# Shift and scale terms of the first norm both as matrix-vector products on TensorE, and the start's low parts and square sums on VectorE

## The reference

```python
def adaln_terms(s, w, b):
    return jnp.split(jax.nn.silu(s) @ w + b, N_MOD, -1)

def modulate(h, g, shift, scale):
    return rmsnorm(h, g) * (1 + scale) + shift

def swiglu(x, w_up, w_down):
    gate, up = jnp.split(x @ w_up, 2, -1)
    return (jax.nn.silu(gate) * up) @ w_down
```

## Time and profile before

| | us |
|---|---|
| three runs, median | 3085.34 |
| lowest, highest | 3085.33, 3086.22 |
| the profiled execution | 3084.96 |
| its span | 3083.2 |
| TensorE busy in it | 2977.2 |
| VectorE, ScalarE, GpSimd busy | 1601.4, 985.1, 997.4 |
| first dense product, start of the steady ones | 25.81, 76.55 |

### The profile page before, as it was taken

One profiled execution on the slowest core, in us unless ns is written; L12 is line 12 of the kernel. 1 busy time (PEld: TensorE's weight loads), 2 busy tenths in 40 slices (PEclk: granted clock), 3 DMA queues, 4 the chain that ended last, 5 costly groups with the idle time before them and its releaser, 6 DMA issues.

```text
span 3083.2 us, 45849 instructions
## 1 busy us (share of the span) xinstructions
PE 2977.2 (97%) x19023; PEld 2788.4 (90%) x19023; DVE 1601.4 (52%) x2437; ACT 985.1 (32%) x1701; POOL 997.4 (32%) x516
## 2 busy tenths in 40 slices
PE   7999999999989988999999999999999999999998
PEld 6999999999888875899999999999999877798997
DVE  6556666784646656477667684212123348431223
ACT  4211212343454457321121232212122247532222
POOL 5333333333332202233333333222222222344442
PEclk8999999999999999999999999999999999999999
DMA  4434454323320022234444342111211210132222
GB/s 189 147 112 133 126 143 130 98 75 125 111 66 15 8 80 78 78 126 137 130 134 145 103 131 69 62 62 59 64 62 55 75 47 2 62 102 90 90 95 70
DMA packets 126236, 284.25 MB, mean 92 GB/s; under 512 B 40222, under 2 KB 57550, under 8 KB 126030
## 3 DMA queue, kind: packets, MB, share of 16 engines
q1 hardware_dynamic: 123150, 274.86, 27.6%
q10 hardware_dynamic: 2880, 6.47, 0.5%
HBM read 269.68 MB, written 15.10 MB: 92 GB/s over the span
## 4 chain that ended last, share of the span: by engine, by line
PE 89%; DVE 5%; ACT 4%; issue 2%; POOL 0%; DMA 0%; ACTq 0%; SPq 0%; DVEq 0%; POOLq 0%
PE psum L1777 78%; PE psum L1952 2%; PE psum L2052 1%; DVE o_acc L1604 1%; PE psum L2040 1%; ACT prob_o L1258 1%; PE psum L2033 1%; PE psum L1937 1%; DVE prob_o L1708 1%; PE psum L1993 1%; PE psum L1972 1%; PE psum L1959 1%; ACT cacc L1112 0%; PE psum L1982 0%; DVE probT_o L1720 0%
## 5 line engine op out<-in xcount | busy, mean ns | idle before, releaser
L883 POOL TENSOR_TENSOR wl<-raw,wh 128x1024 fp32r<-128x1024 f32 (+1 forms) x329 | 838.4, 2548 | 1649.9 <-ACT wh L988 1648.5
L1777 PE MATMUL psum<-uh,wh 128*128 128x256 f32 (+5 forms) x2704 | 661.2, 326 | 24.9 <-DVE ul L1325 14.8
L1777 PE MATMUL psum<-ul,wh 128*128 128x256 f32 (+5 forms) x2704 | 660.6, 325 | 0.0
L1777 PE MATMUL psum<-uh,wl 128*128 128x256 f32 (+5 forms) x2704 | 660.0, 325 | 0.0
L1777 PE MATMUL psum<-ah,wh 128*128 128x386 f32 (+4 forms) x2192 | 595.6, 344 | 5.5 <-POOL wl L883 4.3
L1777 PE MATMUL psum<-ah,wl 128*128 128x386 f32 (+4 forms) x2192 | 591.1, 342 | 0.0
L1777 PE MATMUL psum<-al,wh 128*128 128x386 f32 (+4 forms) x2192 | 588.7, 341 | 0.0
L1777 PEld LDWEIGHTS psum<-uh,wh 128*128 128x128 f32 (+1 forms) x2704 | 451.4, 189 | 49.0 <-issue 23.5
L1529 DVE SCALAR_TENSOR_TENSOR ada_product<-ada_w,cb 128x1024 f32<-128x1024 f32 x256 | 478.1, 1868 | 5.1
L1777 PEld LDWEIGHTS psum<-uh,wl 128*128 128x128 f32 (+1 forms) x2704 | 452.2, 189 | 19.7
L1777 PEld LDWEIGHTS psum<-ul,wh 128*128 128x128 f32 (+1 forms) x2704 | 451.3, 190 | 19.8
(11 more groups left out here) (243 smaller groups left out, 2437.9 us busy)
## 6 DMA issues: line engine op xcount, KB each, us to landing
raw<-in_w SPq DMA_DIRECT2D x264, 512.0 KB, 3.7
ada_w<-in_ada_w SPq DMA_DIRECT2D x128, 512.0 KB, 3.7
raw<-in_w SPq DMA_DIRECT2D x64, 448.0 KB, 3.4
spill<-cacc ACTq DMA_DIRECT2D x16, 384.0 KB, 2.5
scale_w<-in_scale_w SPq DMA_DIRECT2D x8, 512.0 KB, 13.5
ada_start<-in_ada_w SPq DMA_DIRECT2D x8, 512.0 KB, 14.3
ada_w<-bias_final SPq DMA_DIRECT2D x16, 256.0 KB, 3.0
h<-in_xT SPq DMA_DIRECT2D x8, 384.0 KB, 13.7
```

The source lines that it names most:

```text
L883: nc.gpsimd.tensor_tensor(wl[n % SPLIT_SLOTS][:, 0:k * w], raw[n % RAW_SLOTS][:, 0:k * w], wh[n % SPLIT_SLOTS][:, 0:k * w].bitcast(f32), A ...
L1777: ins = nc.tensor.matmul(pair[0:w, lo:hi], wt[n % SPLIT_SLOTS][:, k * w:(k + 1) * w], xt[:, k, cols], start=first, stop=last)
```

## The change

The diff takes the spreading of c out of TensorE's start. The shift term of each feature tile becomes a second matrix-vector product, for both vectors at once, right behind the scale one, from weights laid out as the scale weights are. Its result lies in the second bank of the start's pair, the scale term always in the first, so each product waits until VectorE has read the one before it. `cb`, which the later terms need, is now loaded as a broadcast of c and c_ctx (8 KB spread over 128 partitions, 1 MB written), run through a Sigmoid on ScalarE in the sixth step, and multiplied on VectorE in the seventh. The low parts of the three fused weight tiles and the sums of squares go from GpSimd to VectorE. The scale weights and h get a semaphore each. The identity matrix is loaded on SyncE's queue behind the shift weights, not on ScalarE's at the very start. The numbering of the later modulation chunks loses the first eight.

```diff
             def load_start(k):
-                sp.dma_start(scale_w[k][:, :], a["scale_w"][k]).then_inc(tile_loaded[k], 16)
-                sp.dma_start(h[:, k, :], a["xT"][:, k, :]).then_inc(tile_loaded[k], 16)
+                sp.dma_start(scale_w[k][:, :], a["scale_w"][k]).then_inc(scale_loaded[k], 16)
+                sp.dma_start(h[:, k, :], a["xT"][:, k, :]).then_inc(x_loaded[k], 16)
...
-                sp.dma_start(ada_start[k][:, :], a["ada_w"][ada_order[k]]).then_inc(start_loaded[k], 16)
-            for dst, src in ((mean_w, "mean_w"), (ones_w, "ones_w"), (dn_w, "dn_w")):
+                sp.dma_start(shift_w[k][:, :], a["shift_w"][k]).then_inc(shift_loaded[k], 16)
+            for dst, src in ((mean_w, "mean_w"), (ones_w, "ones_w"), (ident, "ident"), (dn_w, "dn_w")):
...
+            sp.dma_start(cb[:, :, :].rearrange("p v k -> p (v k)"), a["cs"].to_broadcast([P, 2 * D])).then_inc(c_loaded, 16)
...
-                    sp.wait_ge(ada_summed, on_dve(max(ADA_FIRST, n - ADA_BUFS + 1)))
+                    if n >= ADA_BUFS:
+                        sp.wait_ge(ada_summed, on_dve(n - ADA_BUFS + 1))
+                    else:
+                        sp.wait_ge(sc_ready, 3)
...
@@ GpSimd
-            done = [0]
+            done = [FUSED]
...
-            split_up_to(FUSED)
-            for k in range(KD):
-                context_shift(k)
-                if k:
-                    start_square(k - 1)
-            start_square(KD - 1)
...
@@ ScalarE
-            act.dma_start(ident[:, :], a["ident"]).then_inc(ident_loaded, 16)
...
             for k in range(KD):
-                act.wait_ge(tile_loaded[k], 32)
+                act.wait_ge(x_loaded[k], 16)
                 late_high(norm_items[0], k)
-                if k == 0:
-                    act.wait_ge(c_rows_made, 1)
-                    nc.scalar.activation(cb[:, 1, :], c_rows(1), ACT.Copy).then_inc(c_rows_copied[1], 1)
-                act.wait_ge(context_multiplied, k + 1)
-                nc.scalar.activation(context_product[k % 2][:, :], context_product[k % 2][:, :], ACT.Identity,
-                                     accum_out=mod[:, 0, 0, k, 1:2]).then_inc(context_summed, 1)
                 square(0, k)
-                if k == KD - 2:
+                if k == KD - 3:
+                    act.wait_ge(c_loaded, 16)
+                    for v in range(2):
+                        ins = nc.scalar.activation(c_sigmoid[v][:, :], cb[:, v, :], ACT.Sigmoid)
+                    ins.then_inc(sc_ready, 1)
                     act.wait_ge(eps_set, 1)
                     nc.scalar.activation(std[:, 0:1], eps[:, :], ACT.Sqrt)
-                act.wait_ge(start_shift, k + 1)
-                shift_high(0, k, uh).then_inc(shift_hi, 1)
...
@@ late_high, behind the two high halves
+                if m == 0:
+                    act.wait_ge(start_shift, q + 1)
+                    shift_high(m, q, high).then_inc(shift_hi, 1)
...
@@ VectorE
+            def split_low(n):
+                _, k, w = slots[n]
+                dve.wait_ge(hi_split, n + 1)
+                nc.vector.tensor_tensor(wl[n % SPLIT_SLOTS][:, 0:k * w], raw[n % RAW_SLOTS][:, 0:k * w],
+                                        wh[n % SPLIT_SLOTS][:, 0:k * w].bitcast(f32), ALU.subtract).then_inc(lo_split, 1)
...
             def start_shifts(k):
-                dve.wait_ge(ada_summed, k + 1)
-                dve.wait_ge(context_summed, k + 1)
-                nc.vector.tensor_scalar(mod[:, 0, 0, k, :], mod[:, 0, 0, k, :], ada_b[:, 0, 0, k:k + 1], None,
+                dve.wait_ge(start_product_done, 2 * k + 2)
+                nc.vector.tensor_scalar(mod[:, 0, 0, k, :], start_bank(1), ada_b[:, 0, 0, k:k + 1], None,
                                         ALU.add).then_inc(start_shift, 1)
...
+            split_low(0)
             dve.wait_ge(scale_one_set, 1)
             for k in range(KD):
                 start_gains(k)
                 if k == 0:
-                    dve.wait_ge(c_rows_made, 1)
-                    nc.vector.tensor_copy(cb[:, 0, :], c_rows(0)).then_inc(c_rows_copied[0], 1)
-                    dve.wait_ge(c_rows_copied[0], 1)
-                ada_chunk(ada_order[k])
+                    for n in range(1, FUSED):
+                        split_low(n)
+                start_shifts(k)
+                if k:
+                    add_square(0, k - 1)
                 late_low(norm_items[0], k)
-                start_shifts(k)
                 dve.wait_ge(shift_hi, k + 1)
                 shift_low(0, k).then_inc(shift_lo, 1)
-            dve.wait_ge(c_rows_copied[1], 1)
+                if k == KD - 2:
+                    dve.wait_ge(sc_ready, 2)
+                    for v in range(2):
+                        ins = nc.vector.tensor_tensor(cb[:, v, :], cb[:, v, :], c_sigmoid[v][:, :], ALU.mult)
+                    ins.then_inc(sc_ready, 1)
+            add_square(0, KD - 1)
+            dve.wait_ge(sc_ready, 3)
...
@@ TensorE, start_scale(k)
-                if k >= 2:
-                    pe.wait_ge(start_gain, k - 1)
-                pe.wait_ge(tile_loaded[k], 32)
+                if k:
+                    pe.wait_ge(start_gain, k)
+                pe.wait_ge(scale_loaded[k], 16)
                 for q in range(KD):
-                    ins = nc.tensor.matmul(start_bank(k), scale_w[k][:, P * q:P * q + P], c_cols[:, q, :],
+                    ins = nc.tensor.matmul(start_bank(0), scale_w[k][:, P * q:P * q + P], c_cols[:, q, :],
+                                           start=q == 0, stop=q == KD - 1)
+                ins.then_inc(start_product_done, 1)
+                if k:
+                    pe.wait_ge(start_shift, k)
+                pe.wait_ge(shift_loaded[k], 16)
+                for q in range(KD):
+                    ins = nc.tensor.matmul(start_bank(1), shift_w[k][:, P * q:P * q + P], c_cols[:, q, :],
                                            start=q == 0, stop=q == KD - 1)
...
                     start_scale(0)
-                    pe.wait_ge(ident_loaded, 16)
-                    for v in range(2):
-                        for q in range(KD):
-                            ins = nc.tensor.matmul(c_rows(v)[:, P * q:P * q + P], c_cols[:, q, v:v + 1].to_broadcast([P, P]), ident[:, :],
-                                                   start=True, stop=True)
-                    ins.then_inc(c_rows_made, 1)
                     start_scale(1)
-                    for v in range(2):
-                        pe.wait_ge(c_rows_copied[v], 1)
-                    for y in fused:
-                        pe.wait_ge(lo_split, slot_of[y] + 1)
+                    pe.wait_ge(lo_split, FUSED)
```

More of the change, by code:

```diff
@@ L203, in build @@
     plan = ada_plan(items)
-    ada_order = ada_chunks(0, [0]) + [c for i in sorted(plan) for c in plan[i]]
+    ada_order = [c for i in sorted(plan) for c in plan[i]]
     ada_no = {c: n for n, c in enumerate(ada_order)}
-    term_no = {c[:2]: n for n, c in enumerate([c for c in ada_order[ADA_FIRST:] if c[2] == KD - 1])}
-    on_dve = lambda n: n if n <= ADA_FIRST else 2 * n - ADA_FIRST
+    term_no = {c[:2]: n for n, c in enumerate([c for c in ada_order if c[2] == KD - 1])}
+    on_dve = lambda n: 2 * n
     norm_no = {x: i for i, x in enumerate([x for x in items if x[0] == "norm"])}
@@ L281, in build @@
         scale_w = [tb(f"scale_w{i}", [P, D]) for i in range(KD)]
-        ada_start = [tb(f"ada_start{i}", [P, D]) for i in range(ADA_FIRST)]
+        shift_w = [tb(f"shift_w{i}", [P, D]) for i in range(KD)]
         guard.close()
@@ L326, in build @@
         guard.close()
-        start_product, context_product = ada_w[2], ada_w[0:2]
+        c_sigmoid = ada_w[0:2]
         guard, wb = region("deltanet work")
@@ L354, in build @@
         psum = ctx.enter_context(nc.psum_tensor("psum", [P, 4096], f32))
-        ident_loaded, const_loaded = sem("ident_loaded"), sem("const_loaded")
-        c_rows_made, c_rows_copied, context_multiplied, context_summed = (
-            sem("c_rows_made"), [sem(f"c_rows_copied{v}") for v in range(2)], sem("context_multiplied"), sem("context_summed"))
+        x_loaded, c_loaded, const_loaded = [sem(f"x_loaded{i}") for i in range(KD)], sem("c_loaded"), sem("const_loaded")
         c_cols_loaded, terms_loaded = sem("c_cols_loaded"), sem("terms_loaded")
-        tile_loaded = [sem(f"tile_loaded{i}") for i in range(KD)]
+        scale_loaded = [sem(f"scale_loaded{i}") for i in range(KD)]
         c_cols_ready, scale_one_set, start_gain, start_shift = (sem(n) for n in
@@ L364, in build @@
         raw_loaded = [sem(f"raw_loaded{i}") for i in range(RAW_SLOTS)]
-        start_loaded = [sem(f"start_loaded{i}") for i in range(ADA_FIRST)]
+        shift_loaded = [sem(f"shift_loaded{i}") for i in range(KD)]
         ada_loaded = [sem(f"ada_loaded{i}") for i in range(ADA_BUFS)]
@@ L505, in x_before @@
             return [y for y in items[:at] if y[0] in RESIDUAL][-1]
-        CONSTS = 16 * 5
+        CONSTS = 16 * 6
```

(17 more changed lines are left out.)

27 lines of the change are left out of this document (4 added, 23 removed).

## The result

The changed kernel takes 3089.22 us (median of 20 runs, 3084.34 to 3095.88), the one before 3085.39 in the same comparison: a ratio of 1.0014, 95% interval 1.0008 to 1.0019. It is 3.8 us slower, within the 0.2% that the prediction called no difference, and clear of noise with 20 runs of each. The forecast was 3090.7. The profiled execution took 3092.47, 3.3 above the median of its kernel; so it is not the middle of them. One of the 20 runs of the kernel before took 4869.46 us; it is left out of the ratio.

A forecast was written before the change was run, and what follows sets the result against it. TensorE was taken to bound the kernel: 4.2 us gained in front, then 57.7 us of steps at mean clock 0.81, put the norm's product 5.4 us later, hence 3090.7 us; range 3079.5 to 3098.5.

The forecast's parts named there:

- What bounds: Whole kernel: TensorE, busy 97% of the span; a change in the start moves the end equally, tail to 76.55 unchanged.
- steps 1 to 3: Start: GpSimd's work goes; VectorE's 3.0 to 3.6 us per step is hidden; ScalarE's Sigmoids taken as 0, bound +2.
- Ahead of the first dense product: Start: three vector products at 3.41 us from 11.3 put the first dense product at 21.6, 4.2 us gained.
- Work of the steps: Eight steps up to the norm's product: 8 x 3.27 + 6 x 3.42 = 46.7 us at full clock, nothing idle.
- The clock: Eight steps: half-clock share scaled from 0.28 to 0.38, mean 0.81, 57.7 us; norm's product at 79.3, 5.4 us later.
- The rule on idle gaps: Eight steps: with no long idle gap the clock would stay up, norm's product at 70.0; the trace disagreed at 60.2.
- A: Eight steps: the clock stays full once up; norm's product at 70.0, total 3079.7 to 3081.4 us; chance 0.13.
- B: Start: full clock in the steps and the vector products in front; norm's product at 63.3, total 3074.7 us; chance 0.05.
- C: Eight steps: clock falls behind nearly every vector-product pair, mean below 0.80; 3099.7 us with 60% at half; chance 0.34.
- D: Start: VectorE still bounds it, its step exceeding 6.7 us against 3.5 forecast; total 3086 to 3092 us; chance 0.03.

The follow-up runs named there:

- wide version: Changed kernel with every matrix-vector product of the start streaming 128 columns in place of 2: 3076.97 us, ratio 0.9973 to the kernel before.
- shorter shift products: Changed kernel with the shift products of tiles 2 to 7 summing 2 of their 8 parts, leaving work out: 3081.26 us, ratio 0.9988 to the kernel before.
- version wide in front: Changed kernel with 128 columns only in the vector products of tiles 0 and 1, ahead of the first dense product: 3085.25 us, ratio 1.0001.
- interleaved kernel: Changed kernel with the vector products behind steps 0 to 5 cut into single products put between the dense ones, still 2 columns: 3116.15 us, ratio 1.0099.

## Why the prediction was right, step by step

- **What bounds.** Right: all of the difference lies ahead of the steady run, and the tail behind the norm's product is as it was: 2.28 us from the norm's product to the steady run in the chain of either kernel.
- **GpSimd and VectorE (steps 1 to 3).** Right: the low parts, the additions and the waits are hidden. Undoing them changed nothing.
- **Ahead of the first dense product.** 21.6 was worked out, 21.5 measured, and each of the three vector products at 3.4 us. That the half level holds there, against the profile's clock column, is shown by the wide version: its second and third products take 1.78 us.
- **Work of the steps.** 46.7 us at full clock was worked out; the wide version shows 46.9.
- **The clock.** A mean of 0.81 was taken; 0.80 was measured by the column, 0.78 by the pace; the norm's product at 79.3 against 81.2. That the clock takes back the gain in front, and some more, was right. The number came out near, but the scaling behind it does not hold, so its closeness is luck. It let the share at half clock grow with the share of time without dense products. Three runs contradict that. With the same share evenly mixed the clock was never up in the mixed steps; with the share back at about a third (10.3 + 2.6 of 39 us, the shorter shift products) it was still 0.80, where the kernel before has 0.86 at 32%; and in one execution of the version wide in front it was 1.00 for 38.8 us at a share of 44%. How the work lies in time matters as well, and something that differs between executions of one kernel.
- **The rule on idle gaps.** The prediction weighed the Trainium skill, "TensorE: Matmul & The Clock Gate", section "Why this matters for your kernels", which asks for no long idle gaps between bursts of matmuls. The changed kernel has no idle gap at all from 21.5 to 81.2, and a mean clock of 0.80; by that rule alone the norm's product would have come at 70.0. The trace disagrees. With the same passes and 128 columns in each the clock stayed at 1.00; the wide version differs in nothing else.
- **Rivals.** A (the clock stays up) is what the wide version does by other means, 65.1, and what single executions of others show for most of the steps; for the changed kernel it did not come in the profile and its fastest run, 3084.34, is still 3 us above A's upper edge. B fell. C, a mean below 0.80, is the edge at which the profiled execution stood (7.5 us more than the one profiled before); the median stayed 2.4 us short of it. D fell: VectorE was busy 20 of 60 us.

What stays open is which property of the vector products, their share or the length of a stretch of them, brings a fall, and why executions of one kernel differ by up to 11 us. The granted clock differs between profiled executions in the start, and in the body too (3002.4 to 3008.9 us behind the start); for the executions without a profile there is no trace. The prediction did not speak of this spread, and its single number could have been any between 3084 and 3096.

## What to carry to other kernels

Work moved to TensorE is not priced by its passes alone: a matrix-vector product there streams next to no columns, and dense products behind it can run at half pace. If such products can't be avoided, try giving them more columns (here 128 in place of 2 cost at most 0.1 us per 16 passes and won 12 us), and look at the granted clock of the stretch before and after. And look at who sets the pace first: the same cure did nothing for the kernel before, whose steps waited for VectorE.

## What the runs showed of the hardware

- 16 passes with 128 moving columns take 1.78 us, with 2 columns 1.68 to 1.79: the time hardly depends on the columns. That the weight load of each pass sets it is likely, since it is what both have alike, but no run varies it.
- Evenly mixed dense and 2-column products from a start at the half level ran at that level for over 75 us, with TensorE busy without a gap.
- From the start of a trace up to its first fall the clock's column reads 1.00, whatever the pace. In the interleaved kernel it does so through 75 us of half pace:

```profile
21.30:100.00 78.70, 78.70 (x310) 78.70 (x311) 20.40 (x51) 17.32 (x37) 0.00 (x0) 1.00 0.26 101
```

The distance from one product to the next tells the level there.
- A fall costs little where another engine sets the pace: in the kernel before, two falls of 3.4 us went, and the norm's product came 0.4 us earlier.
- The clock can differ between executions of the same work: at 2500 to 2600 us, behind starts that were alike, it was 1.00 in one profile and 0.97 in another.
